# TensorE's order in one slot of a hybrid decoder step: scores, turns and value product ahead of the projection pieces

## What is computed

```python
p = x @ w_in                                   # x: 560 x 2048 in all, w_in: 2048 x 6664
k_past = cache_k[page_table]                   # 8 sequences x 4096 keys x 8 heads x 128
v_past = cache_v[page_table]
z = einsum('bqhd,bkhd->bhqk', q, k_all) * SB_SCALE + bias      # stick-breaking attention
log_keep = where(mask, log_sigmoid(-z), 0)
log_pass = cumsum(log_keep, reverse=True) - log_keep
a = where(mask, exp(log_sigmoid(z) + log_pass), 0)
h_att = einsum('bhqk,bkhd->bqhd', a, v_all)
```

## The kernel before

| what | slots |
|---|---|
| two chunks in the slot | 4, 8, 12, 17, 21, 25, 30, 34, 38, 42, 47, 51, 55, 60, 64, 68, 72 (one in all others) |
| a pair ends in the slot | -13, -9, -5, -1, 3, 6, 9, 12, 16, 19, 22, 25, 29, 32, 35, 38, 42, 45, 48, 51, 55, 58, 61, 64, 68, 71; the gates in 72 |
| of these, the pair ends with the first of two chunks | 42, 55, 68 |
| first slot of a batch (`probabilities`, `queries`, `stick`) | 0, 8, ..., 56 (64 for `probabilities` and `stick` alone) |
| turns of a batch | 9, 17, ..., 65 |

## Time and profile before

### The profile page before, as it was taken

How to read it: one execution, slowest core, us unless ns; L and a number is a source line. 1 busy time by engine, 2 the same in 40 slices (tenths; PEclk the granted TensorE clock), 3 DMA queues, 4 the chain that set the end, 5 groups by cost and what they waited for, 6 DMA issues and landing times. The chain is left out here.

```text
span 3279.4 us, 60260 instructions
## 1 busy us (share of the span) xinstructions
PE 2967.9 (90%) x26582; PEld 2790.9 (85%) x26582; DVE 1381.4 (42%) x1518; ACT 705.4 (22%) x913; POOL 237.6 (7%) x231
## 2 busy tenths in 40 slices
PE   5998898989999576689979999999999999999995
PEld 5997787878888355469979999999999999999995
DVE  2264445354541684452363333333333333333335
ACT  2221112122211441121152221222122112212211
POOL 0011111110100420000130000000000000000002
PEclk8999899999999786689989999999999999999997
DMA  8479999999987521024412223222222332222222
GB/s 316 131 284 390 362 355 393 362 391 369 379 336 256 163 82 48 22 62 136 137 51 86 83 89 91 90 80 89 91 82 87 91 90 82 87 91 78 90 91 81
DMA packets 332633, 547.39 MB, mean 167 GB/s; under 512 B 17545, under 2 KB 237362, under 8 KB 322578
## 3 DMA queue, kind: packets, MB, share of 16 engines
q1 hardware_dynamic: 310882, 385.00, 35.3%
q0 software_dynamic: 13872, 143.43, 10.8%
q10 hardware_dynamic: 7632, 15.20, 1.2%
HBM read 507.75 MB, written 35.83 MB: 166 GB/s over the span
## 5 line engine op out<-in xcount | busy, mean ns | idle before, releaser
L324 PE MATMUL prj_G<-prj_xh,prj_wh 128*128 128x280 f32 x1696 | 510.8, 301 | 27.9 <-DVE prj_wl L538 27.9
L326 PE MATMUL prj_G<-prj_xh,prj_wl 128*128 128x280 f32 x1696 | 503.6, 297 | 0.0
L325 PE MATMUL prj_G<-prj_xl,prj_wh 128*128 128x280 f32 x1696 | 503.4, 297 | 0.0
L545 DVE STREAM_TRANSPOSE prj_kT<-prj_k_nat 128x4096 f32<-128x4096 f32 x64 | 284.4, 4444 | 350.3 <-PE prj_S L357 350.3
L324 PEld LDWEIGHTS prj_G<-prj_xh,prj_wh 128*128 128x128 f32 x1696 | 328.9, 194 | 57.2 <-issue 30.6
L1344 PE MATMUL big_G<-big_mh,wh 128*128 128x272 f32 x1216 | 352.9, 290 | 18.7 <-issue 9.6
L1345 PE MATMUL big_G<-big_ml,big_wh 128*128 128x272 f32 x1248 | 359.5, 288 | 0.0
L1344 PE MATMUL big_G<-big_mh,big_wh 128*128 128x272 f32 x1248 | 359.2, 288 | 0.0
L1346 PE MATMUL big_G<-big_mh,big_wl 128*128 128x272 f32 x1248 | 358.2, 287 | 0.0
L1345 PE MATMUL big_G<-big_ml,wh 128*128 128x272 f32 x1216 | 351.7, 289 | 0.0
L1346 PE MATMUL big_G<-big_mh,wl 128*128 128x272 f32 x1216 | 350.9, 289 | 0.0
(11 more groups left out here) (349 smaller groups left out, 5311.5 us busy)
## 6 DMA issues: line engine op xcount, KB each, us to landing
prj_v_nat<-in_cache_v SPq DMA_DIRECT2D x256, 512.0 KB
raw<-in_w_up SPq DMA_DIRECT2D x64, 1024.0 KB, 6.4
raw<-in_w_down SPq DMA_DIRECT2D x64, 1024.0 KB, 5.0
prj_raw<-in_w_in SPq DMA_DIRECT2D x106, 512.0 KB
raw<-in_w_out SPq DMA_DIRECT2D x16, 1024.0 KB, 6.2
prj_scratch<-prj_stage ACTq DMA_DIRECT2D x53, 280.0 KB
out_xr<-x_scratch SPq DMA_DIRECT2D x16, 544.0 KB, 6.9
mix_att<-prj_scratch SPq DMA_DIRECT2D x24, 280.0 KB, 3.4
```

What stands on the lines that cost most here:

```text
L324: mm(out, w_hi[:, k, m], xh[:, k0 + k, cols], start=(first and k == 0), stop=False)
L325: mm(out, w_hi[:, k, m], xl[:, k0 + k, cols], start=False, stop=False)
L326: last = mm(out, w_lo[:, k, m], xh[:, k0 + k, cols], start=False, stop=(end and k == nk - 1))
L545: V.transpose(flat(kT[:, :, :, :, :].rearrange("p r h b i -> p r (h b i)")), flat(k_nat[k % 2][:, :, :]))\
```

## The change

In the loop over the slots, TensorE's program runs the scores of the slot first, then the second half of the turns, the turn of an output, and the value product, and the projection's chunks last. The first half of the turns stays at the head of the slot. The lists of the other engines are as before.

```diff
                 b, s = divmod(k - LAG, NSTEP)
                 if b >= 0 and s == 0:
                     turn(b, 0)
-                for n in chunks_of(k):
-                    chunk(n)
+                if 0 <= k < NB * NSTEP:
+                    scores(k)
                 if b >= 0 and s == 0:
                     turn(b, 1)
                 if b > 0 and s == 1:
                     turn_output(b - 1)
-                if 0 <= k < NB * NSTEP:
-                    scores(k)
                 if b >= 0:
                     weigh(k - LAG)
+                for n in chunks_of(k):
+                    chunk(n)
             turn_output(NB - 1)
```

## The result

The changed kernel took 3338.1 us (median of 4 runs, 3336.6 to 3342.1) against 3281.4 for the kernel before on the same chip (4 runs, three of them the ones listed above): a ratio of 1.0171 (95% interval 1.0147 to 1.0195), 57 us slower. The forecast had the sign, but it said 33 us, and the result lies outside its range. The profiled execution took 3342.13 us, its span 3340.3.

What follows compares the result with a forecast made beforehand. It took PE to bound the phase at both ends, PE and fetches together the middle. Costs less cheaper turns summed to +37.4 us, less 4 given back: +33 on 3281.3, stated as 3314 after a 1.6 us median adjustment; range 3298 to 3326.

Steps and rivals of the forecast that it cites:

- A: Slot 0: scores wait for the queries, which ACT lays out after copying out a pair and issuing its stores; 5.3 us.
- B: Slot 4, after a pair ends in slot 3: PE waits for the transpose behind copy, high and low parts; 7.4 us.
- D: Slot 30, after a pair ends in slot 29: PE waits for the transpose behind copy, high and low parts; 7.4 us.
- C: Slot 17: `stick` also precedes the transpose; PE waits 11.7 us, 7.4 more than before.
- Smaller ones: Slots 8, 25, 56 and 57: short waits of PE behind late chains of ACT and DVE; 4.1 us together.
- Cheaper turns: Two short waits of the turns go, since the turns come after a chunk more; 1.1 us saved.
- the end: End of the phase: the last value product no longer runs beside the copy and store chain; 1.8 us added.
- That costs nothing where the others need only an older chunk: All slots: every chunk comes one slot later, priced at nothing unless the next scores need that slot's chunk.
- the 4 us: Slots 9 to 63: waits for the transpose let fetches catch up, shortening later waits for values; 4 us back.
- rival (4): Exposed chains disturb the value loads; waits for values grow by 7 us, giving 3322 to 3328; chance 0.1.
- lower clock: After the bare waits in slots 0, 4 and 30: part of the work runs at 1.2 GHz; 1.7 us each, 5.1 us.
- weighed rule: Middle slots: a 358 GB/s limit would hide PE's waits there and make the sum +19; rejected, since 419 was moved.

Runs made afterwards that it cites:

- Values first: The changed kernel with SP's list of a slot turned round, the two half steps of values before the weights: 3316.7 us, ratio 1.0124.
- high parts first: The changed kernel with ACT's list turned round, high parts of the next slot's chunks before the copies out of a finished pair: 3309.3 us, ratio 1.0099.
- values late in the old one: The kernel before, with SP loading weights one slot further ahead in 14 slots, so that value loads stand behind them: 3311.4 us, ratio 1.0099.
- values first in it: The kernel before with SP's list alone turned round, values ahead of weights: 3288.4 us, ratio 1.0031.
- both edits: The changed kernel with SP's values before its weights and ACT's high parts before its copies out of a pair: 3277.1 us, ratio 0.9998.
- all lists in step: The changed kernel with SP values before weights, ACT high parts before copies, DVE transpose, cumulative product, then low parts: 3276.7 us, ratio 0.9999.
- transpose first: The changed kernel with SP's values before weights and DVE's key transpose ahead of low parts and cumulative product: 3299.3 us, ratio 1.0070.
- high parts late in the kernel before: The kernel before, PE's order untouched, with ACT's high parts made to wait for a chunk about one slot later: 3307.6 us, ratio 1.0098.

## Why the prediction was wrong

The sign, the place and most single terms were right. By its steps:

- **A, B, D** (5.3, 7.4, 7.4): 5.16, 7.29, 7.29 us of waiting, by the chains named. **C** (11.7, 4.28 of it paid before): 7.88 + 3.24 = 11.1. **Smaller ones**: slot 8 0.9 (1.3 said), slot 57 1.0 (1.2), slot 56 nothing (0.1), slot 25 nothing (1.5), since slot 24 waited 3.8 us for values and the transpose was done meanwhile. **Slots 0 to 8** in all: 105 us with one chunk (6.2) less in them, against 93.7, so 17.5 lost; 17.4 was said.
- **Cheaper turns and the end** came as said. Missed: the second half of the turns of slot 65, which has no scores to cover ACT's copy, 1.7 us, and 0.7 of waits for values in the last slots; some 3 of the 24 us that the forecast lacks.
- **The step that failed** is the sentence "That costs nothing where the others need only an older chunk", with the 4 us that were to be given back in the middle. Slots 9 to 63 lost 35.3 us (756.1 against 720.8), and 14.2 was said. PE's idle time grew by 20.8 and not by about 12: the waits for values rose by 7 instead of falling by 4. The other 14.5 us are work of PE that took longer; 1.7 was said. The granted clock in the middle fell from 0.95 to 0.93. The 4 us rested on a misread row besides: the window 533 to 553 of the earlier trace rows starts at the scores of slot 30, behind both of its chunks, and holds one chunk each of slots 31 and 32, so it says nothing of slots with two.
- **What the runs showed in its place.** The forecast looked for chains that end at the next scores and priced late low parts at nothing wherever no such chain came out. But others than PE need the low parts too: a weight load waits for the low part in SP's queue, and value loads are queued behind. Values first took 21 us off the middle; beside high parts first, where no bare wait is left, it took 29; and making value loads late in the kernel before cost 34. The forecast did see SP's queue at D and asked there alone. What it said of that place held: the loads went out 4.0 us after the chunk's end (558.74 against 554.7; 3 was said), and slot 30 had no wait for values. But they were 17.2 us late against the product that frees their buffer, and whether that cost anything in later slots no run tells by itself. Its rival (4), disturbed value loads, was the right mechanism, at 7 to 14 us and a chance of 0.1, and tied to slots like D instead of to all of them. Its 7 us happen to be what the list of waits rose by (76.2 against 68.7), but the middle cost 21 us more than forecast, three times that.
- **Of the lower clock** the runs say that it goes with PE's idle time in the middle, whatever ends it: 0.93 with 95 us (the changed kernel, and values late in the old one), 0.94 and 0.95 with 84 and 85 (high parts first, values first), 0.95 with 74 and 78 (before, and values first in it), 0.96 with 61 and 62 (both edits, all lists in step). Two stand out of the row: 71 us at 0.94 (transpose first) and 76 at 0.94 (high parts late in the kernel before). The stretches at 1.2 GHz after the bare waits were priced; that more waits for values bring more of them was not. This goes together in the runs; none sets the clock apart from the waits.
- **The weighed rule.** The Trainium skill's 358 GB/s (DMA: Bandwidth & Descriptors, Bandwidth), by which the middle would have been bound by fetches and the change cheaper, is no limit for this kernel: 379 GB/s over 708 us in the kernel with both edits. The same section says that about 358 is each core's share when both cores of a pair stream, and this kernel ran on one core. That part of the forecast held.

What is open: how far late transposes, which also delay the fetch of keys, cost anything. In the kernel with both edits they lag by 75 us in all and in the one with all lists in step by 8, and the two take the same time, so here it is little. Why a middle of 708 us instead of 721 (both edits against the kernel before) doesn't make that kernel faster is plain: slots 0 to 8 give 8 us of it back and the end 4. Why the middle itself is 13 us shorter is not shown; its waits for values are 9 us less than before, although the value loads were all but on time in both (late by 2 and 6 us in all). And each trace is one execution: the part of the program behind this phase, which no edit touches, took from 2207 to 2218 us in them, so differences of 5 us between two traces say little.

## What to carry to other kernels

When one engine's order changes, what it signals comes at other times, and every queue that waits for it must be asked, not only for what the engine itself needs next but for what stands behind the waiting entry: here a DMA queue with two kinds of loads in one fixed order. A list of loads should be in the order in which the consumer needs them; each of the two orders of PE had its own better order for SP, and the other one cost 10 us in the old and 15 to 32 in the new. A quick sign in a profile is which of its waits a DMA queue stands at: 61 us at the weight load before, 329 after. It is a hint and no proof: with high parts late in the old order it was 327, with the value loads all but on time. What decides is how long after the release of its buffer a load goes out.

## What was not expected of the hardware

The same loads came at 364 GB/s over 737 us or at 379 over 708, by the order of SP's list alone (high parts first, without and with values first). And a few microseconds of lateness were dear for TensorE twice: of the 35 us lost in the middle, 14 were not waiting but work that took longer, at a mean granted clock of 0.93 instead of 0.95.
